# A product-key expert stage: query and expert tiles in three rounded passes, with GpSimd making the remainders

## The reference, cut to what matters

```python
def block(hb):                      # hb: the normed rows
    q = (hb @ w_pq).reshape(TOK_BLOCK, PEER_HEADS, 2, PEER_DHALF)      # 8 heads, 2 x 128
    s = jnp.einsum('thpd,hpnd->thpn', q, sub_keys)
    s1, i1 = lax.top_k(s[:, :, 0], 16); s2, i2 = lax.top_k(s[:, :, 1], 16)
    cand_s = s1[..., :, None] + s2[..., None, :]          # 256 candidates a head
    top_s, pos = lax.top_k(cand_s, 16); idx = take(cand_i, pos)
    gate = softmax(top_s)
    act = gelu(einsum('thkd,td->thk', expert_u[idx], hb))
    return einsum('thk,thkd->td', gate * act, expert_v[idx])
```

## Time and profile before

| | us |
|---|---|
| median of 3 runs | 2259.36 (2258.87 to 2261.01) |
| the profiled execution | 2254.98 |
| its span | 2253.2 |
| TensorE busy | 2172.7 (96%) |
| VectorE busy | 1471.9 (65%) |
| ScalarE busy | 1020.5 (45%) |
| GpSimd busy | 40.4 (2%) |

### The profile page before, as it was taken

The page is one execution under the profiler, slowest core; times in us unless marked ns, Lnnn a source line. Parts: engine busy times, 40 slices in busy tenths (PEclk is TensorE's granted clock), DMA queues, the critical chain, the costliest instruction groups (busy, mean ns, idle before and its releaser), DMA issues.

```text
span 2253.2 us, 42372 instructions
## 1 busy us (share of the span) xinstructions
PE 2172.7 (96%) x15414; PEld 1947.1 (86%) x15428; DVE 1471.9 (65%) x2790; ACT 1020.5 (45%) x1734; POOL 40.4 (2%) x40
## 2 busy tenths in 40 slices
PE   8999999999999999999998879999999999999999
PEld 7998997899889977899897547889888999999998
DVE  5557996655645556655675555989887666666665
ACT  4335775433433446433551343337634444444443
POOL 0000000000000000000000000110000000000000
PEclk9999999999999999999999989999999999999999
DMA  6555653455475534455431014443576666655554
GB/s 215 186 188 176 215 170 124 159 193 178 158 279 185 194 114 143 160 193 177 162 92 32 19 52 140 146 141 141 179 240 225 215 213 205 206 187 187 185 188 137
DMA packets 107550, 377.28 MB, mean 167 GB/s; under 512 B 11760, under 2 KB 17664, under 8 KB 107072
## 3 DMA queue, kind: packets, MB, share of 16 engines
q1 hardware_dynamic: 102848, 354.88, 47.7%
q0 software_dynamic: 4608, 21.15, 3.0%
HBM read 362.29 MB, written 13.69 MB: 167 GB/s over the span
## 4 chain that ended last, share of the span: by engine, by line
PE 88%; DVE 6%; ACT 2%; DMA 2%; DVEq 1%; issue 1%; ACTq 0%; POOL 0%; SPq 0%
PE bank L350 68%; PE bank L379 8%; PE bank L2495 3%; PE bank L1609 3%; DVE u_lo L565 1%; DVE w_lo L302 1%; DMA ring<-in_w 1%; ACT w_hi L297 1%; PE bank L598 1%; PE bank L616 0%; PE bank L2126 0%; DMA ring<-in_ssm_in 0%; DVE arena L1980 0%; DMA ring<-in_rwkv_in 0%; PE bank L876 0%
## 5 line engine op out<-in xcount | busy, mean ns | idle before, releaser
L302 DVE TENSOR_TENSOR w_lo<-ring,w_hi 128x1024 fp32r<-128x1024 f32 x581 | 702.6, 1222 | 423.2 <-ACT w_hi L297 420.5
L297 ACT ACTIVATE w_hi<-ring 128x1024 fp32r<-128x1024 f32 x581 | 605.9, 1057 | 635.1 <-PE bank L350 555.1
L350 PE MATMUL bank<-u_hi,w_hi 128*128 128x256 f32 x2568 | 730.7, 285 | 9.1 <-DVE w_lo L302 9.1
L350 PE MATMUL bank<-u_lo,w_hi 128*128 128x256 f32 x2568 | 728.4, 284 | 0.0
L350 PE MATMUL bank<-u_hi,w_lo 128*128 128x256 f32 x2568 | 728.4, 284 | 0.0
L350 PEld LDWEIGHTS bank<-u_hi,w_hi 128*128 128x128 f32 x2568 | 493.9, 192 | 20.3 <-DVE w_lo L302 8.0
L350 PEld LDWEIGHTS bank<-u_lo,w_hi 128*128 128x128 f32 x2568 | 494.1, 192 | 7.4 <-issue 0.5
L350 PEld LDWEIGHTS bank<-u_hi,w_lo 128*128 128x128 f32 x2568 | 494.0, 192 | 0.0
L350 PE MATMUL bank<-w_hi,x_hi 128*128 128x512 f32 x992 | 392.1, 395 | 8.2 <-DVE x_lo L1087 4.0
L350 PE MATMUL bank<-w_lo,x_hi 128*128 128x512 f32 x992 | 390.1, 393 | 0.0
L350 PE MATMUL bank<-w_hi,x_lo 128*128 128x512 f32 x992 | 387.6, 391 | 0.0
(11 more groups left out here) (312 smaller groups left out, 1758.9 us busy)
## 6 DMA issues: line engine op xcount, KB each, us to landing
ring<-in_w SPq DMA_DIRECT2D x264, 512.0 KB, 3.6
ring<-in_expert_u SPq DMA_DIRECT2D x128, 512.0 KB, 3.5
ring<-in_expert_v SPq DMA_DIRECT2D x128, 512.0 KB, 4.2
ring<-in_ssm_in SPq DMA_DIRECT2D x40, 512.0 KB, 4.4
gate_dram<-con SPq DMA_DIRECT2D x16, 576.0 KB, 2.8
arena<-gate_dram POOLq DMA_DIRECT2D x9, 1024.0 KB, 8.7
ring<-in_ssm_out SPq DMA_DIRECT2D x16, 512.0 KB, 3.8
ring<-in_w_o SPq DMA_DIRECT2D x16, 512.0 KB, 3.7
```

What stands on the lines that cost most here:

```text
L297: act.activation(w_hi[slot][:, :], ring[slot][:, :], ACT.Copy).then_inc(hi_made[slot], 1)
L302: dve.tensor_tensor(w_lo[slot][:, :], ring[slot][:, :], w_hi[slot][:, :].bitcast(F32), ALU.subtract).then_inc(freed[slot], 1)
L350: mm = pe.matmul(out, left[a], right[b], start=start and n == 0, stop=stop and n == 2, skip_group_check=True)
```

## The change

The 16 query tiles and 32 of the expert tiles of the peer stage (16 beside the heads, 16 gate tiles) go from plain products to three rounded passes. ScalarE rounds each; GpSimd makes each remainder (except the first, which VectorE makes). The loads are issued in another order, `u_t` isn't made in this norm, and in six norms (`POOL_LEADS`) GpSimd in place of VectorE makes the second lead tile's remainder. The diff, cut to its core:

```diff
@@ -178,21 +178,23 @@
     "peer_b": ((NKEYS - PRE) // 2, [1, 1, 1, 1]),
 }
 SPLIT_STAGES = ("ffn0", "ffn1", "ffn2", "ffn3", "ssm", "rwkv", "peer")
-PLAIN_STAGES = ("attn", "peer")
+PLAIN_STAGES = ("attn",)
 LOG_AND_EXP = "natural_log_exp_and_others"
 OUT_RINGS = ("ssm_out", "attn_out", "mix_out")
 TABLE_KEPT = ("ffn1", "ffn3", "peer")
 LEAD_BEFORE = {"ssm": 1, "ffn1": 2, "ffn2": 1, "ffn3": 1, "rwkv": 1}
 LEAD_AFTER_ROOTS = ("ffn3",)
+POOL_LEADS = ("ssm", "ffn1", "ffn2", "ffn3", "rwkv", "peer")
 SSM_CLOSE_SLOTS = (1, 2, 3, 0, 1, 2, 3, 0, 1, 2, 0, 3, 1, 0, 2, 3)
 FIRST_CONSTS = 4 * P
-SPLIT_RINGS = SPLIT_STAGES + ("mla", "peer_v", "peer_b") + OUT_RINGS
+SPLIT_RINGS = SPLIT_STAGES + ("mla", "route", "gate_u", "peer_v", "peer_b") + OUT_RINGS
 RING_OF = {"ssm": ("ssm", "ssm_out"), "attn": ("attn", "attn_out"), "mla": ("mla", "mla_heads"), "mix": ("mix_out",),
            "peer": ("route", "gate_u", "peer_v", "peer_b")}
 
 LEAD = {**{f"ffn{k}": [(0, f"ffn{k}"), (1, f"ffn{k}"), (2, f"ffn{k}")] for k in range(4)},
         "ssm": [(n, "ssm") for n in range(4)],
-        "rwkv": [(n, "rwkv") for n in range(4)]}
+        "rwkv": [(n, "rwkv") for n in range(4)],
+        "peer": [(n, "route") for n in range(4)]}
 STAGES = ["ffn0", "ssm", "ffn1", "ffn2", "kv", "attn", "ffn3", "rwkv", "mla", "mix", "peer"]
 
 
@@ -536,15 +538,9 @@
                 ins.then_inc(S("u_turned"), 1)
                 if s == stages[0]:
                     lead_scalar(act, s, slice(0, 1) if q == 1 else slice(1, None))
-            if split and s in PLAIN_STAGES:
-                act.wait_ge(S("u_made"), 2 * m + 2)
-                for q in range(4):
-                    if q % 2:
-                        act.wait_ge(S("u_turned"), 2 * m + q // 2 + 1)
-                    act.activation(quarter(u_hi, q), quarter(u_t, q), ACT.Copy).then_inc(S("u_t_split"), 1)
 
         def norm_vector(dve, s):
-            m, split = norm_no[s], s in SPLIT_STAGES
+            m = norm_no[s]
             gain = GAIN[s]
 
             def rows(tt):
@@ -573,14 +569,6 @@
                 rows(1)
                 turned(0, u_t)
                 turned(2, u_t)
-            elif s in PLAIN_STAGES:
-                turned(0, u_t)
-                rows(1)
-                turned(2, u_t)
-                for q in range(4) if split else ():
-                    dve.wait_ge(S("u_t_split"), q + 1)
-                    dve.tensor_tensor(quarter(u_lo, q), quarter(u_t, q), quarter(u_hi, q).bitcast(F32),
-                                      ALU.subtract).then_inc(S("u_split"), 1)
             else:
                 if s == stages[0]:
                     dve.wait_ge(S("in_loaded"), 32)
@@ -588,7 +576,8 @@
                 rows(1)
                 turned(2, u_hi)
                 dve.drain()
-                lead_vector(dve, s, slice(0 if s == stages[0] else 1, 2))
+                if s not in POOL_LEADS:
+                    lead_vector(dve, s, slice(0, 2))
                 for q in (0, 2, 1, 3):
                     lo(q)
 
@@ -2379,8 +2368,9 @@
             def v_first(j, i):
                 load(sp, V_SLOTS[j], io["expert_v"][bass.ds(4 * i + j, 1), :, :], "peer_v", i)
 
-            def pre(n, i):
-                load(sp, 2 + n, io["expert_u"][bass.ds(2 * i + n, 1), :, :], "route", i)
+            def pre(i):
+                for n in range(2):
+                    load(sp, 2 + n, io["expert_u"][bass.ds(2 * i + n, 1), :, :], "route", i)
 
             def under_gates(g):
                 if g < GATE_U:
@@ -2399,24 +2389,22 @@
                              staged[c % 2].rearrange("p e t -> p (e t)")).then_inc(S(f"gates_stored{c % 2}"), 16)
 
             queries(0)
+            pre(0)
             sp.wait_ge(S("h_updated"), 4 * upd["peer"] + 1)
             sp.dma_start(keys_all.rearrange("p (h n) -> p h n", h=PH), io["keys"].rearrange("h p n -> p h n")).then_inc(S("table_loaded"), 16)
             with sp.Fori(0, PH - 1) as i:
                 queries(i + 1)
-                pre(0, i)
-                pre(1, i)
-            pre(0, PH - 1)
-            pre(1, PH - 1)
+                pre(i + 1)
             under_gates(0)
             v_first(0, 0)
             under_gates(1)
             v_first(1, 0)
-            for g in range(2, UNDER_TURN + 2):
+            for g in range(2, UNDER_TURN + 4):
                 under_gates(g)
             for c in range(NCHUNKS):
                 for k in range(4 * c - 2, 4 * c + 2):
-                    if k in TILE_AFTER:
-                        under_gates(TILE_AFTER[k] + 2)
+                    if k in TILE_AFTER and TILE_AFTER[k] + 4 < GATE_U + 2:
+                        under_gates(TILE_AFTER[k] + 4)
                 store(c)
             with sp.Fori(0, PRE // 4 - 1) as i:
                 for j in range(4):
@@ -2435,8 +2423,7 @@
             def queries(i):
                 pe.wait_ge(S("pq_out"), 2 * i + 2)
                 for n in range(2):
-                    arrived(pe, n, "route", i)
-                    project(pe, ROT[n][:, 0:T], n, fresh="peer" if i == n == 0 else None).then_inc(freed[n], 1)
+                    project_split(pe, ROT[n][:, 0:T], n, "route", i)
 
             def head(i, more=True):
                 pe.wait_ge(S("pq_out"), 2 * i + 4)
@@ -2450,18 +2437,15 @@
                 if more:
                     queries(i + 1)
                 for n in range(2):
-                    arrived(pe, 2 + n, "route", i)
                     pe.wait_ge(S("pre_gelu"), 2 * i + n + 1)
-                    project(pe, bank[(2 * i + n) % 4][:, 0:T], 2 + n).then_inc(freed[2 + n], 1)
+                    project_split(pe, bank[(2 * i + n) % 4][:, 0:T], 2 + n, "route", i)
 
             def gate_tile(g):
-                slot, stage, i, nth = gate_slot(g)
-                arrived(pe, slot, stage, i, nth)
                 pe.wait_ge(S("pre_gelu"), ROUTE_PRE + g + 1)
-                project(pe, bank[(ROUTE_PRE + g) % 4][:, 0:T], slot).then_inc(freed[slot], 1)
-
+                project_split(pe, bank[(ROUTE_PRE + g) % 4][:, 0:T], *gate_slot(g))
+
+            project_first(pe, "peer", *((ROT[0][:, n * T:(n + 1) * T], n, "route", 0, 0) for n in range(2)), one_bank=True)
             pe.wait_ge(S("table_loaded"), 32)
-            queries(0)
             for i in range(PH):
                 head(i, more=i < PH - 1)
             for g in range(AT_CHOICE):
@@ -2474,7 +2458,6 @@
             for g in range(AT_CHOICE, UNDER_TURN):
                 gate_tile(g)
             pe.wait_ge(S("choice_ready"), 2)
-            u_split_ready(pe, "peer")
 
             def up(n, i):
 
@@ -2515,13 +2498,24 @@
 
         def peer_scalar(act):
             def queries(i):
+                if not i:
+                    split_done(act, 1, "route", 0)
                 for n in range(2):
-                    multiplied(act, n, "route", i)
-                    act.activation(pq_t[:, n, :], ROT[n][:, 0:T], ACT.Copy).then_inc(S("pq_out"), 1)
+                    split_done(act, n, "route", i)
+                    src = ROT[n][:, 0:T] if i else ROT[0][:, n * T:(n + 1) * T]
+                    act.activation(pq_t[:, n, :], src, ACT.Copy).then_inc(S("pq_out"), 1)
+
+            def next_queries(i):
+                if i + 1 < PH:
+                    for n in range(2):
+                        make_hi(act, n, "route", i + 1)
+                else:
+                    make_hi(act, *gate_slot(0))
 
             def head(i, more=True):
                 if more:
                     queries(i + 1)
+                    next_queries(i + 1)
                 else:
                     tiles(i)
                     for g in range(AT_CHOICE - 1):
@@ -2534,8 +2528,12 @@
 
             def tiles(i):
                 for n in range(2):
-                    multiplied(act, 2 + n, "route", i)
+                    split_done(act, 2 + n, "route", i)
                     pre(2 * i + n)
+                    if i + 1 < PH:
+                        make_hi(act, 2 + n, "route", i + 1)
+                    elif n == 0:
+                        make_hi(act, *gate_slot(1))
 
             def scores(i):
                 act.wait_ge(S("score_done"), i + 1)
@@ -2545,10 +2543,13 @@
                 act.activation(pre_gelu[:, j:j + 1, :], bank[j % 4][:, 0:T].unsqueeze(1), ACT.Gelu).then_inc(S("pre_gelu"), 1)
 
             def gate_tile(g):
-                multiplied(act, *gate_slot(g))
+                split_done(act, *gate_slot(g))
                 pre(ROUTE_PRE + g)
+                if g + 2 < GATE_U:
+                    make_hi(act, *gate_slot(g + 2))
 
             queries(0)
+            next_queries(0)
             scores(0)
             for i in range(PH):
                 head(i, more=i < PH - 1)
@@ -2608,10 +2609,23 @@
             step(1, bodies_b - 1, ahead=False, more=False)
 
         def peer_pool(pool):
+            lead_vector(pool, "peer", slice(2, None))
+            for n in range(2):
+                make_lo(pool, n, "route", 1)
             for i in range(PH):
```

(15 more changed lines are left out.)

## The result

The changed kernel takes 2307.44 us (median of 5 runs, 2301.76 to 2309.05), the kernel before 2259.36 (5 runs, 2258.79 to 2261.01): ratio 1.0204, 95% interval 1.0186 to 1.0221. It is slower by 48.1 us; 44.3 were predicted. The profiled execution spans 2300.1 us against 2253.2.

The account below looks back on a forecast made before the run. TensorE was taken to bound the heads, by less than half a microsecond over VectorE. Heads with start +28.2, turn +10.5, gates +11.7, norms -6.1 made +44.3: 2259.4 + 44.3 = 2303.7 us, range 2272 to 2316.

Parts of the forecast that it names:

- The start: Program start to head 0's score copy: -8.7 us, with VectorE beginning head 0 about 2.6 us earlier and the norms' -6.1.
- The heads: Head 0 to head 7: 133.7 us against 102.9, so +30.8 us.
- The mutual wait: Heads: VectorE and GpSimd, each reading two SBUF tiles, wait for each other; 20.1 us a head instead of 18.7.
- ring of 20.1 us: Heads: slot loads, ScalarE's rounding and GpSimd's five operations follow one another, 18.7 us, plus 1.2 + 0.1 for held marks.
- so VectorE isn't in the ring: Heads: VectorE's marks come at 4.6 us of the next turn, before the pick at 11.3, so VectorE doesn't set the head.
- The turn: Last pick to the gates: remainder, load, rounding, table load and exponent follow the pick, 8.8 us later; +10.5 with mutual waits.
- Half of 10 x 2.35: Gates: ten GpSimd remainders each stop VectorE's one-hot rows up to 2.35 us; half was taken, +11.7 us.
- the gain is gone: 0: Gates: ScalarE's 11 roundings use up TensorE's 6.5 us gain, so 0 before hold-ups (bounds -6.5, +1).
- The five norms: ssm, ffn1, ffn2, ffn3 and rwkv: GpSimd makes VectorE's 1.23 us remainder while `u_hi` is made, -6.1 us.
- the ring without mutual waits: Rival 1: the heads' chain of loads at 18.7 us a head, no hold-ups; +21.2, 2280.6 us; chance 0.30.
- the ring doesn't close: Rival 3: in the heads loads don't hold up GpSimd, VectorE bounds them; -9.6, 2249.8 us; chance 0.05.
- rival 2: VectorE's single-tile gate operations wait too, +9, 2313 us, or TensorE's clock falls in the heads' gaps; chance 0.08.

Follow-up runs that it names:

- leads_only: The kernel before, with GpSimd in place of VectorE making the second lead tile's remainder in five norms; 2251.23 us, ratio 0.9975.
- leads_and_keys: leads_only, with TensorE's wait for the keys put behind head 0's two query tiles; 2248.76 us, ratio 0.9961 to the kernel before.
- fills_in_place: load_order, with GpSimd filling each remainder's buffer with zeros, reading nothing, in place of the subtraction; 2261.01 us, ratio 1.0016 to the kernel before.
- one_tile_read: load_order, with GpSimd writing one tile times zero in place of the subtraction; 2273.51 us, ratio 1.0073 to the kernel before.
- load_order: The changed kernel, with SyncE issuing slots 0 and 1 one head further ahead of slots 2 and 3; 2300.77 us, ratio 1.0196 to the kernel before.
- turn_2: The changed kernel, with gate tile 1's remainder before the last pick and one gate tile fewer ahead of the last exponent; 2300.80 us, ratio 1.0193.

## Why the prediction was right

**The start (-8.7, measured -9.7).** Right in its two causes, and the sum lies close by luck. The last norm begins 7.9 us sooner and S0 follows 1.8 us faster, where 2.6 was the term. Of the 7.9 us, 5.2 are the five remainders by leads_only. The other 2.7 fall into the stages between 1093 and 1365 us, whose length differs by more from one execution to the next: from the norm at about 1095 to the next it takes 244 us here, 247 in the kernel before and 252 in leads_and_keys, where the clock is 0.94 for 0.97. They are not counted as the change's, which leaves it 7.0 us.

**The heads (+30.8, measured +30.0).** The size was right, the working only half. The mutual wait is real, and choosing it over its absence was right: fills_in_place takes it away and with it the heads' whole loss, and one_tile_read, with GpSimd as busy as before, most of it. The ring of 20.1 us is also there, 20.3 where it closed, with a landing of 6.5 us for 5.3. What failed is the step "so VectorE isn't in the ring", which let the marks alone be held up, by 1.3 us, and had "the candidates (L2661) slip under slack". VectorE has 0.46 us of slack a head, and its products, casts and scalar operations that meet a GpSimd remainder wait for up to the whole of it: 18 rows in seven heads, of which the marks are two and account for 4.0 of the 33.5 us. That puts VectorE itself at 18.7 us with the loads well ordered and at about 19 as they are (14.24 + 33.5 / 7). Two limits, 20.1 and 19, happened to lie about 1 us apart, and so the wrong one gave the right number. That was luck. The prediction's own sign speaks against its ring: the MAX8 rows are 18 to 22 us apart, but ScalarE's copy released them once in the window and not in each head. GpSimd's wait for `w_hi` did come, 6.9 us a time, but it is there under either limit. load_order is what tells them apart: by the prediction's ring it should have freed the heads, and it gave back 5.8 us of 30.

**The turn (+10.5, measured +13.6).** Right in its chain, step for step. From the end of the pick to VectorE's next row it is 9.8 us for 8.8, because TensorE's tile, counted as lying under the load, took 4.39 us and not 2.9: the granted clock was 0.67 over that stretch. Hold-ups before the pick took 2.5 us for 1.7. The last 1.3 us are TensorE's and ScalarE's steps behind it.

**The gates (+11.7, measured +13.0).** Near in size, with two terms that were mis-sized in opposite ways. "Half of 10 x 2.35" for the hold-ups: the rows grew by 122 x (453 - 342) + 61 x (520 - 419) ns = 19.7 us, about 2 us for each remainder, of which VectorE's spare time took 9 to 10; without them the stretch is 9.8 us shorter. "Part of each stop falls on the 0.51 us in which it reads one tile" was wrong: those rows (L2737) were held most of all. And "the gain is gone: 0" was +3.2. In the windows TensorE's clock is 0.98 here and in fills_in_place, and 1.00 in the earlier trace rows; the first 24 products took 4.54 us, where they took 2.92 in turn_2. That may be half of the 3.2 us; the rest stays open.

**The five norms (-6.1).** By leads_only 5.2 in the trace and 5.8 in the medians.

**The rivals.** The stretched rows rule out the ring without mutual waits (2280.6). The rival that the ring doesn't close (2249.8) is out as well; with its hold-ups gone, fills_in_place does run the heads at VectorE's pace, as that rival had it, but with load_order's queue, so it says nothing on the ring in the changed order. Of rival 2 the half on single-tile operations holds, with half its price taken up by VectorE's spare time, and the clock does fall in the heads, to 0.86, without setting them: TensorE was busy for 93.51 of 132 us.

## What to carry to other kernels

GpSimd is not a free third pair of hands for VectorE's work. Before moving an operation to it, count the VectorE rows that will run beside it: a product, cast or scalar operation may be held for as long as a two-tile GpSimd operation lasts, and so the place to use it is where VectorE reads one operand from the matmul results, as in the five norms, or reduces or searches. Saving 0.59 us a tile on the bound engine is worth nothing where the neighbour has 0.46 us of slack; ask first for each engine's own time per head, with what the change adds to its neighbours. And where a queue in order feeds a ring of buffers, look at which load stands behind which wait: two slots loaded one head earlier in SyncE's order gave back 6 us.

## What the runs showed of the hardware

A GpSimd subtraction that reads two 128x1024 tiles holds up VectorE's products of two tiles, casts and scalar operations, and short ones cost as much as long ones: a TENSOR_SCALAR on 32 uint32 elements took 2.35 us instead of 0.17 (at 1430.72), a CAST of 64 elements 1.73 to 2.27 instead of 0.20. MAX8, the searches, the replacements and TENSOR_REDUCE kept their lengths, and so did the rows of leads_only that read one operand from `bank` (0.69 us). The other way round two GpSimd remainders of 4.7 us together became 5.70. The Trainium skill (SBUF — State Buffer, Who interferes with whom) says that VectorE with two SBUF inputs, or in its doubled modes for casts and tensor_scalar, shares a port pair with GpSimd, that whoever comes second waits for the whole instruction, and that reductions never contend. The changed kernel's rows agree, the single-input ones too. one_tile_read differs: beside a GpSimd operation of 2.77 us with one input, a two-tile product of VectorE (128x512) took its usual 0.68 us, one of 128x32 took 0.61 for 0.19, and a cast was held for 0.8, so not for the whole instruction; there the measurement decides.
